# Attention probabilities of four heads divided by their sums in one VectorE operation instead of four

## The reference, cut to what matters

```python
scores = jnp.where(mask[None, :, None, None], scores, -jnp.inf)
m = jnp.maximum(scores.max(axis=-1), sink)
e = jnp.exp(scores - m[..., None])
probs = e / (e.sum(axis=-1) + jnp.exp(sink - m))[..., None]
o = jnp.einsum('bnkgqs,bnskd->bnqkgd', probs.astype(v.dtype), vb)
```

## Time and profile before

| | |
|---|---|
| three runs, median (lowest to highest) | 1142.06 us (1140.66 to 1142.89) |
| the profiled execution, its own time | 1143.35 us |
| its span, first to last instruction | 1141.6 us |
| PE busy | 1107.6 us, 97% of the span |
| DVE busy | 765.5 us, 67% |
| ACT busy, POOL busy | 453.7 us, 252.9 us |
| the 128 divisions (L1316) | 42.9 us of VectorE, 43.8 to 299.4 us plus the last one's length |
| mean granted TensorE clock | 0.993 of full speed |

### The profile page before, as it was taken

How to read it: one execution, slowest core, us unless ns; L and a number is a source line. 1 busy time by engine, 2 the same in 40 slices (tenths; PEclk the granted TensorE clock), 3 DMA queues, 4 the chain that set the end, 5 groups by cost and what they waited for, 6 DMA issues and landing times.

```text
span 1141.6 us, 15063 instructions
## 1 busy us (share of the span) xinstructions
PE 1107.6 (97%) x5418; PEld 930.1 (81%) x5418; DVE 765.5 (67%) x1129; ACT 453.7 (40%) x796; POOL 252.9 (22%) x230
## 2 busy tenths in 40 slices
PE   7899999998999996999999999999999999999998
PEld 6788888886888885888888888888888888888887
DVE  5788887888553588766766676668777774564321
ACT  5565666566432314233223323553333332243100
POOL 6532322323100185324532450000000000010000
PEclk9999999999999998999999999999999999999999
DMA  7000000013142404332533234899888882111211
GB/s 277 20 19 20 18 18 18 18 34 151 38 153 87 148 19 166 148 145 114 203 148 144 115 133 144 340 408 345 286 293 289 291 287 77 38 37 56 84 40 44
DMA packets 61801, 154.41 MB, mean 135 GB/s; under 512 B 5040, under 2 KB 6064, under 8 KB 61744
## 3 DMA queue, kind: packets, MB, share of 16 engines
q1 hardware_dynamic: 61600, 153.12, 37.4%
q10 hardware_dynamic: 144, 0.52, 0.1%
HBM read 119.55 MB, written 34.08 MB: 135 GB/s over the span
## 4 chain that ended last, share of the span: by engine, by line
PE 80%; DVE 10%; POOL 3%; ACT 3%; issue 3%; DMA 0%; ACTq 0%; DVEq 0%; POOLq 0%
PE pair L1997 23%; PE pair L1976 23%; PE pair L2040 8%; PE pair L1859 6%; PE pair L1731 5%; PE pair L2017 4%; ACT probs L895 2%; PE pair L1799 2%; PE pair L2053 2%; PE pair L1770 2%; DVE probs L1298 2%; DVE probs L1316 1%; PE pair L1936 1%; PE pair L1906 1%; PE pair L1782 1%
## 5 line engine op out<-in xcount | busy, mean ns | idle before, releaser
L1997 PE MATMUL pair<-uT 128*128 128x512 f32 x1176 | 266.7, 389 | 0.0
L1997 PEld LDWEIGHTS pair<-uT 128*128 128x128 f32 x1176 | 220.7, 188 | 45.8
L1126 ACT ACTIVATE uT<-wo_raw 128x1024 fp32r<-128x1024 f32 x63 | 63.9, 1053 | 105.0 <-PE pair L1997 89.4
L638 POOL TENSOR_SCALAR row_var<-row_ssq 128x1 f32<-128x1 f32 x24 | 4.6, 192 | 437.0 <-ACT hn L1023 430.3
L1572 DVE TENSOR_TENSOR uT<-wo_raw,uT 128x1024 fp32r<-128x1024 f32 x63 | 74.8, 1221 | 39.5 <-ACT uT L1126 39.5
L1731 PE MATMUL pair<-WA,xT 128*128 128x512 f32 x384 | 96.4, 401 | 1.4 <-DVE kn L1255 1.0
L1859 PE MATMUL pair<-WA,oT 128*128 128x512 f32 x384 | 91.6, 396 | 2.3 <-DVE WA L1374 1.7
L1859 PEld LDWEIGHTS pair<-WA,oT 128*128 128x128 f32 x384 | 72.4, 191 | 17.6 <-issue 1.9
L1731 PEld LDWEIGHTS pair<-WA,xT 128*128 128x128 f32 x384 | 70.7, 191 | 17.4 <-issue 2.9
L895 ACT ACTIVATE probs<-probs,nmax 128x257 f32<-128x257 f32 x128 | 63.7, 500 | 52.3 <-DVE nmax L1303 52.1
L1976 PE MATMUL pair<-WA,WB 128*128 128x512 f32 x312 | 74.4, 396 | 3.6 <-ACT xr L1101 3.6
(11 more groups left out here) (182 smaller groups left out, 2074.7 us busy)
## 6 DMA issues: line engine op xcount, KB each, us to landing
wo_raw<-in_m_w SPq DMA_DIRECT2D x53, 512.0 KB, 6.5
wo_raw<-hid_kept SPq DMA_DIRECT2D x36, 512.0 KB, 4.6
hid_kept<-RES SPq DMA_DIRECT2D x28, 512.0 KB, 2.6
emb<-in_m_w SPq DMA_DIRECT2D x20, 512.0 KB, 6.5
RES<-in_m_w SPq DMA_DIRECT2D x8, 1024.0 KB, 6.7
RES<-in_a_wqkv SPq DMA_DIRECT2D x12, 512.0 KB, 8.8
uT_f<-in_m_w SPq DMA_DIRECT2D x6, 1024.0 KB, 6.7
act_buf<-hid_kept SPq DMA_DIRECT2D x11, 512.0 KB, 4.6
```

Source lines behind the costliest of these rows:

```text
L1126: nc.scalar.activation(operand(t, which, HI), unit(t, which), ACT.Copy).then_inc(op_hi, 1)
L1997: mm = nc.tensor.matmul(ps[4 * (j % 2) + m][:], operand(t, 0, s)[:, k, m * P:(m + 1) * P], operand(t, 1, r)[:, k, :], start=(g == 0 and k ...
```

## The change

The four multiplications of a step, one for each head, each with a scalar per partition (`rden[:, i, r:r + 1]`), become one multiplication of two tensors: the [128, 4, 256] part of `probs`, and `rden` [128, 4] repeated over 256 elements by a zero step. The number of elements is the same. The waits before it, the place in the order and the semaphore after it stay.

```diff
             def scale_probs(n, j):
                 t, i = 4 * n + j, j % 2
                 dve.wait_ge(rden_ready, t + 1)
-                for r in range(G):
-                    ts = nc.vector.tensor_scalar(probs[:, i, r, 0:2 * P], probs[:, i, r, 0:2 * P], rden[:, i, r:r + 1],
-                                                 None, ALU.mult)
-                ts.then_inc(probs_ready, 1)
+                row = probs[:, i, :, 0:2 * P]
+                nc.vector.tensor_tensor(row, row, rden[:, i, :].unsqueeze(2).to_broadcast([P, G, 2 * P]),
+                                        ALU.mult).then_inc(probs_ready, 1)
```

## The result

The changed kernel takes 1143.79 us (median of 17 runs, 1142.30 to 1144.65) against 1142.04 us before (17 runs, 1140.66 to 1143.14). The ratio is 1.0014, 95% interval 1.0007 to 1.0020 (0.8 to 2.3 us): slower by 1.75 us. That is less than the 0.2% that I had called about what can be told, but with 17 runs each the interval leaves no change out. The forecast was 1143.8 us, from 1142.06 + 1.75.

What follows compares the result with a forecast made beforehand. PE bounds the kernel, waiting for VectorE between attention blocks. Terms of 0.07 (block 0), 1.32 (blocks 1 to 6) and 0.36 (block 7) give 1.75 us on 1142.06: 1143.8 us, 8-in-10 range 1142.0 to 1145.9.

Steps and rivals of the forecast that it cites:

- PE waits for VectorE before blocks 2 to 7: Before each of these blocks PE stands still 0.4 to 0.6 us for VectorE's keys; the gap grows by 0.22 us.
- An undisturbed division costs +0.08: Merged operation takes 1.22 us; what follows at once starts 1.14 instead of 1.06 us after the first start.
- rival B: The new form is dearer than plain rows, by zero step or row spacing; at 1.29 us, 1145.0 us; chance 0.13.
- Behind the copy +0.15, and +0.07 by the end of step 3: Blocks 1 to 6: step 2 waits for GpSimd's key copy, 1.00 for 0.85 us; step 3 adds 0.07; together 1.32 us.
- rival A: GpSimd does not hold the new operation, so the kernel gets faster by 4.4 us, 1137.7 us; chance 0.07.
- Step 1 is swallowed and step 0 is not on the way, in blocks 1 to 6: Step 1's 0.07 us vanishes in step 2's wait for the key copy; step 0 ends before 0.67 us of VectorE idle time.
- Block 7: 0.36: Last attention block: all four divisions pay, 0.13 us in step 0, then 0.07, 0.08 and 0.08.
- Block 0: 0.07: First attention block: only step 1's division pays, 0.07 us; the two after it do not, as PE has no gap.
- GpSimd is held 0.8 us and nobody waits: Behind step 1's division GpSimd's chain runs 0.8 us late, at no cost, under a cover of 0.3 + 1.19 us.
- rival C: GpSimd's lateness outgrows its cover, beyond 1.5 us of delay; 0.2 us a block, 1.2 us more, 1145.0 us; chance 0.06.
- Rival D: The old group moves elements at twice the new one's rate; 18 us lost over the divisions, 1160 us; chance 0.02.
- The low clock: After PE's idle time until 451.9 us, a stretch mostly at 1.2 instead of 2.4 GHz costs up to 1.7 us.

Runs made afterwards that it cites:

- The plain tile: Changed kernel with a plain tile as second input in blocks 1 to 5, leaving the division out there: 1144.5 us in one execution, blocks 32.97 us apart.
- the moved copy: GpSimd's key copy of blocks 1 to 6 held until step 2's division ends: 1138.33 us on the kernel before, 1139.64 us on the changed kernel.

## Why the prediction was right

The forecast's 1.75 us were measured as 1.75. That the two agree to the digit is luck: the interval is 0.8 to 2.3 us, and the trace shows 1.95, since the term for block 0 was too small. The steps are what carries it, and one of them failed.

- **PE waits for VectorE before blocks 2 to 7.** The six gaps grew from 0.56 to 0.73 us on average (I had said near 0.8), and the blocks by 0.22. Shown by the distances, and by the run in which the gap closes when VectorE's way gets shorter.
- **An undisturbed division costs +0.08.** 1.14 against 1.06 us to the next start. The price of the form (rival B) was bounded from above by 1.29 and taken at 1.22; it is 1.226. The plain tile shows that neither form adds to it.
- **Behind the copy +0.15, and +0.07 by the end of step 3.** 0.99 against 0.85 us, and 1.26 against 1.18; 1.33 us for six blocks against 1.32. Rows 6 spoke against rival A before the run, and the moved copy settles it.
- **Step 1 is swallowed and step 0 is not on the way, in blocks 1 to 6.** Shown by the new form in steps 0 and 1 alone: no change of these blocks.
- **Block 7: 0.36.** 0.37 in the trace.
- **Block 0: 0.07** failed; it is 0.25. Step 1 costs 0.08 there, as forecast. But I had left steps 2 and 3 out, "since PE goes into block 1 without a gap". No gap does not mean room. The keys were ready 0.03 us at most before PE wanted them, and 0.17 of the loss of the two steps comes through. The run with the new form in steps 2 and 3 alone shows it (+0.15), and so does the one with four two-tensor operations, where a wait of 0.54 us opens at that place. Nineteen divisions pay, not seventeen.
- **GpSimd is held 0.8 us and nobody waits.** L645 took 1.00 us, and the cover (put at 0.3 + 1.19) was 0.47 + 1.20 after the delay. I had not foreseen that the sink placement after the copy is held too; it has some 10 us until it is needed. The extra operations show where rival C begins: with one more, of 1.64 us, no block grows; with two, 2.65 us together, the blocks grow by 0.22.
- **Rival D** needed an old group twice as fast. What the chip does shows in the four two-tensor operations: the kinds differ by 0.28 us a group, neither by twice nor by nothing.
- **The low clock** as scatter of up to 1.7 us: in the profiled pair it made the spans equal. A reader who had only the spans would have called the change free.

Not tried: whether an operation with one input in PSUM would escape GpSimd. All eight banks are in use by PE in attention, and a shared bank would need new waits.

## What to carry to other kernels

Fewer operations are not a gain by themselves: here three starts saved gave 0.20 us and the slower kind took 0.28. Price both, from the next start and not only from the duration, and then look at what GpSimd does at the same moment: its key copy cost each block more (0.66 us) than the choice between the two forms of the division (0.22), and one wait that moves it is worth 3.4 us. An engine that does not wait can still have nothing to spare: look for how long before its start the thing it needs was ready. When differences are below the scatter of a run, compare the distances between repeated points in the trace, and add no tile to a test kernel without keeping the later ones in place.

## What had not been expected of the hardware

Moving the tiles behind a pad by 96 bytes a partition made the kernel 11.4 us slower (1.0081 to 1.0115), with no other edit. Products that read one moved tile and one that had not moved took 5 to 9 ns more (396 instead of 389 in the groups shown); products with both inputs from the moved tile (1176 of them) stayed at 389. Why the relative place matters is not settled by these runs. And the place of a stretch at a low granted clock hid a loss of 1.5 us entirely in one pair of profiled executions.
